# A bidirectional chunked scan: both directions' intra-chunk products in the first pass, the second pass with the state alone

## The reference, cut to what matters

```
xd    = x * dt[..., None]
a_cs  = cumsum(dt * a)                                   # in the chunk
decay = exp(where(tri, a_cs[l] - a_cs[s], -inf))
cb    = einsum("bclgn,bcsgn->bclsg", cc, bc)
y_diag = einsum("bclsgr,bcsgrp->bclgrp", cb * decay, xd) # inside a chunk
states = einsum(..., bc, exp(a_cs[-1] - a_cs), xd)       # what a chunk adds to the state
h      = h * exp(a_cs[-1]) + states                      # chunk after chunk
y_off  = einsum(..., cc, h_prev, exp(a_cs))              # what earlier chunks give
```

## Time and profile before

| | us |
|---|---|
| median of 3 runs | 4335.32 (4332.63 to 4337.5) |
| the profiled execution, its time | 4333.42 |
| its span | 4331.6 |
| `ssd_stage` in it, first to last instruction | 383.3 to 559.7 |

### The profile page before, as it was taken

One profiled execution on the slowest core, in us unless ns is written; L12 is line 12 of the kernel. 1 busy time (PEld: TensorE's weight loads), 2 busy tenths in 40 slices (PEclk: granted clock), 3 DMA queues, 4 the chain that ended last, 5 costly groups with the idle time before them and its releaser, 6 DMA issues. The chain is left out here.

```text
span 4331.6 us, 38016 instructions
## 1 busy us (share of the span) xinstructions
PE 3116.2 (72%) x12308; PEld 1334.8 (31%) x12308; DVE 2859.9 (66%) x7086; ACT 1130.9 (26%) x2975; POOL 1575.2 (36%) x1383
## 2 busy tenths in 40 slices
PE   8999999866667755555566658999877655555655
PEld 4656554422222211111122113565332211111111
DVE  2524765898888897555555555565888888555554
ACT  1122532333223222111222212563332322111111
POOL 0001413354554454444444441001445455444443
PEclk9999999988878887778778778999888877777677
DMA  4114858999999999999999994105999999999998
GB/s 175 39 39 138 276 187 319 390 420 415 420 420 399 420 421 420 419 421 414 410 419 418 420 417 190 39 1 199 395 420 420 416 421 417 421 421 419 419 421 336
DMA packets 223658, 1471.81 MB, mean 340 GB/s; under 512 B 25436, under 2 KB 29244, under 8 KB 53220
## 3 DMA queue, kind: packets, MB, share of 16 engines
q0 software_dynamic: 184320, 1342.26, 75.0%
q1 hardware_dynamic: 37764, 123.17, 7.9%
q10 hardware_dynamic: 1376, 3.96, 0.2%
HBM read 1467.02 MB, written 2.28 MB: 339 GB/s over the span
## 5 line engine op out<-in xcount | busy, mean ns | idle before, releaser
L1944 PE MATMUL banks<-arena 128*64 128x512 f32 x5120 | 1668.5, 812 | 1159.2 <-ACT arena L2188 1108.6
L1668 POOL DMA_INDIRECT arena<-experts,arena x1280 | 1498.9, 1171 | 2246.5 <-PE banks L1944 1535.3
L2341 DVE CUSTOM_DVE_ANT_0 arena<-arena 128x1024 f32<-128x1024 f32 x1280 | 1537.4, 1223 | 829.5 <-DMA arena<-experts,arena 828.9
L1944 PEld LDWEIGHTS banks<-arena 128*64 128x64 f32 x5120 | 457.5, 185 | 2297.1 <-ACT arena L2188 1295.1
L2182 ACT ACTIVATE arena<-arena 128x4 f32<-128x4 f32 x320 | 66.1, 206 | 2316.9 <-DVE arena L2341 2316.8
L2188 ACT ACTIVATE arena<-arena 128x64 f32<-128x64 f32 x1280 | 340.4, 336 | 37.5 <-DVE arena L2329 0.8
L1759 PE MATMUL banks<-arena 128*128 128x512 f32 (+3 forms) x960 | 289.4, 456 | 6.8 <-DMA arena<-wq 5.7
L442 PE MATMUL banks<-arena 128*128 128x512 f32 (+1 forms) x640 | 208.6, 486 | 0.3 <-PEq L207 0.3
L1759 PEld LDWEIGHTS banks<-arena 128*128 128x128 f32 x960 | 160.8, 191 | 116.3 <-issue 90.8
L879 POOL TENSOR_TENSOR arena<-arena 128x256 f32<-128x256 f32 x48 | 41.1, 856 | 423.5 <-POOLq L633 332.3
L1686 PE MATMUL banks<-arena 128*128 128x512 f32 x416 | 187.9, 600 | 5.9 <-DVE arena L2234 2.1
(11 more groups left out here) (245 smaller groups left out, 2970.5 us busy)
## 6 DMA issues: line engine op xcount, KB each, us to landing
arena<-l_w_ada SPq DMA_DIRECT2D x48, 1024.0 KB, 4.9
arena<-wq SPq DMA_DIRECT2D x54, 512.0 KB, 7.9
arena<-experts,arena POOLq DMA_INDIRECT x1280, 17.3
arena<-l_w_in SPq DMA_DIRECT2D x7, 2048.0 KB, 7.7
arena<-l_w_out SPq DMA_DIRECT2D x4, 1536.0 KB, 8.9
arena<-l_w_o SPq DMA_DIRECT2D x4, 1024.0 KB, 9.2
arena<-keys SPq DMA_DIRECT2D x27, 128.0 KB, 10.4
arena<-gates SPq DMA_DIRECT2D x6, 512.0 KB, 11.9
```

Source lines behind the costliest of these rows:

```text
L1668: pool.indirect_dma_start(slots[n], None, tbl, bass.IndirectOffsetOnAxis(ap=expert[:, ring[c], k:k + 1], axis=0)).then_inc(land[n]["sem"], ...
L1944: mm = pe.matmul(core["ps"][QS * j:QS * j + QS, c, :], diag[:, g % 2, k, :], v[:, D + c * 512:D + (c + 1) * 512], start=(g % (NB * PH) == ...
L2341: dve.tensor_tensor_reduce(u, u, rep[i // PH % 2][:, k % NQ, :], 1.0, 0.0, ALU.mult, ALU.add, dots[:, k:k + 1]).then_inc(dot["sem"], up(dot))
```

## The change

`steps` keeps its 48 entries, and the first 24 (the backward pass) now make the intra-chunk products of both directions; the forward pass is left with the state.

- `front(n)` exists for the 24 steps of the first pass only, is issued two steps ahead, and has one matmul of scores and two of sums, one per direction, into banks 0 and 1. Each bank has one buffer, so each waits for ACT's distance of the step before.
- ACT's `distance(n)` makes four Relu for each direction, into E (three buffers) and EF (one). The two distances are zero on opposite sides of the diagonal. POOL's `both(n)` adds them over 128x512, and ACT's `decay(n)` is then one Exp for both.
- DVE's `mask(n)` masks the scores twice. ACT's `scale_backward(n)` multiplies the backward scores by dt for four heads (Copy with a scale per partition). DVE's `weigh(n)` makes forward scores·dt + that (four SCALAR_TENSOR_TENSOR of 128x128), and one product with E in place. XD is gone: the product takes x itself.
- XE is x·(TOE·dt), with TOE·dt formed once on POOL at the start; closing steps make none.
- In the forward pass a step has the product with the state, the new state (into banks 2 and 3 in turn) and `add` without its last part.
- Four column groups are now done in the first pass, in six steps each (2, 1, 2, 1, 2 slices and the turn); the fifth has a slice in every other step of the forward pass, and is turned in step 40.

```diff
-    assert len(groups) * (KD + 1) <= NS
+    share = (2, 1, 2, 1, 2)
+    ada_at = {n: [] for n in range(NS)}
+    for q in range(len(groups) - 1):
+        for a, w in enumerate(share):
+            ada_at[6 * q + a] = [(q, sum(share[:a]) + b) for b in range(w)]
+        ada_at[6 * q + len(share)] = [(q, KD)]
+    for k in range(KD + 1):
+        ada_at[NW + 2 * k] = [(len(groups) - 1, k)]
...
+            def distance(n):
+
+                _r, t, g = steps[n]
+                for j, r in enumerate((1, 0)):
+                    act.wait_ge(fr["sem"], at(fr, 2 * n + j + 1))
+                    if j == 0 and n >= 3:
+                        act.wait_ge(bk["sem"], at(bk, n - 2))
+                    if j == 1 and n:
+                        act.wait_ge(ds_["sem"], at(ds_, n))
+                    o = EF if j else E[:, n % 3, :]
+                    for h in range(HG):
+                        c = r * HEADS + g * HG + h
+                        i = act.activation(o[:, h * P:(h + 1) * P], core["ps"][:, j, h * P:(h + 1) * P],
+                                           ACT.Relu, bias=KAC[:, t, c:c + 1], scale=-1.0)
+                    i.then_inc(dd["sem"], up(dd))
+
+            def scale_backward(n):
+
+                _r, t, g = steps[n]
+                act.wait_ge(cm["sem"], at(cm, 2 * n + 1))
+                if n:
+                    act.wait_ge(wg["sem"], at(wg, n))
...
+                    i = act.activation(SB[:, h * P:(h + 1) * P], CM[:, 2 * (n % 2), :], ACT.Copy,
+                                       scale=DT[:, t, c:c + 1])
+                i.then_inc(bs["sem"], up(bs))
+
+            def decay(n):
+
+                act.wait_ge(ds_["sem"], at(ds_, n + 1))
+                act.activation(E[:, n % 3, :], E[:, n % 3, :], ACT.Exp, scale=-1.0).then_inc(eo["sem"], up(eo))
+
+            distance(0)
+            scale_backward(0)
+            distance(1)
+            decay(0)
+            scale_backward(1)
+            for n in range(NS):
+                if n + 1 < NW:
+                    decay(n + 1)
+                if n + 2 < NW:
+                    distance(n + 2)
+                    scale_backward(n + 2)
...
+            def weigh(n):
...
+                for h in range(HG):
+                    c = g * HG + h
+                    i = dve.scalar_tensor_tensor(
+                        out=W[:, h * P:(h + 1) * P], in0=CM[:, 2 * (n % 2) + 1, :], scalar=DT[:, t, c:c + 1],
+                        in1=SB[:, h * P:(h + 1) * P], op0=ALU.mult, op1=ALU.add)
+                i.then_inc(wg["sem"], up(wg))
+                dve.wait_ge(wg["sem"], at(wg, n + 1))
                 dve.wait_ge(eo["sem"], at(eo, n + 1))
...
+                dve.tensor_tensor(E[:, n % 3, :], E[:, n % 3, :], W, ALU.mult).then_inc(mo["sem"], up(mo))
...
             mask(0)
+            mask(1)
+            weigh(0)
             for n in range(NS):
-                if n + 1 < NS:
-                    mask(n + 1)
+                if n + 2 < NW:
+                    mask(n + 2)
+                if n + 1 < NW:
+                    weigh(n + 1)
                 add(n)
...
+            def both(n):
+
+                pool.wait_ge(dd["sem"], at(dd, 2 * n + 2))
+                pool.tensor_tensor(E[:, n % 3, :], E[:, n % 3, :], EF, ALU.add).then_inc(ds_["sem"], up(ds_))
+
+            both(0)
+            both(1)
             for n, (r, t, g) in enumerate(steps):
...
+                if not closing[n]:
+                    c = r * HEADS + g * HG
+                    pool.tensor_tensor(per(XE[:, n % 2, :]), per(xs[:, t, g * GW:(g + 1) * GW]),
+                                       bcast(TOE[:, t, c:c + HG], HD), ALU.mult).then_inc(xe["sem"], up(xe))
+                if n + 2 < NW:
+                    both(n + 2)
...
             def front(n):
...
+                for j, r in enumerate((1, 0)):
+                    e = r * SG + g
+                    if n:
+                        pe.wait_ge(dd["sem"], at(dd, 2 * n - 1 + j))
+                    pe.matmul(core["ps"][:, j, :].rearrange("p (h l) -> p h l", l=P),
...
             front(0)
+            front(1)
             for n, (r, t, g) in enumerate(steps):
-                if n + 1 < NS:
-                    front(n + 1)
+                if n + 2 < NW:
+                    front(n + 2)
                 if n == 0:
                     stay_busy(pe, core, 6, 22)
...
+                if n < NW:
+                    pe.wait_ge(mo["sem"], at(mo, n + 1))
+                    for h in range(HG):
+                        a = g * GW + h * HD
+                        pe.matmul(core["ps"][:, 4 + n % 2, h * HD:(h + 1) * HD], E[:, n % 3, h * P:(h + 1) * P],
+                                  xs[:, t, a:a + HD], start=True, stop=True)
...
+                    pe.wait_ge(xe["sem"], at(xe, n + 2 - sum(closing[:n])))
+                    if 0 < n < NW:
                         pe.wait_ge(ac["sem"], at(ac, AC[n]))
```

More of the change, by code:

```diff
@@ L779, in _ @@
         def _(act):
[L780 to L783, removed]
-                for h in range(HG):
[L785 to L790, removed]
+            def distance(n):
[12 more added lines that the diff above has]
+                    i.then_inc(dd["sem"], up(dd))
@@ L840, in add @@
                             out=part(hs, h), in0=part(hs, h), scalar=CD[:, t, c + h:c + h + 1],
-                            in1=part(core["ps"][:, 6, 0:GW], h), op0=ALU.mult, op1=ALU.add)
+                            in1=part(state, h), op0=ALU.mult, op1=ALU.add)
                     i.then_inc(ac["sem"], up(ac))
-                if not opening[n]:
-                    dve.wait_ge(ac["sem"], at(ac, AC[n] + 1))
-                dve.tensor_tensor(yg, yg, core["ps"][:, 4 + n % 2, 0:GW], ALU.add).then_inc(ac["sem"], up(ac))
+                if n < NW:
+                    if not opening[n]:
+                        dve.wait_ge(ac["sem"], at(ac, AC[n] + 1))
+                    dve.tensor_tensor(yg, yg, core["ps"][:, 4 + n % 2, 0:GW], ALU.add).then_inc(ac["sem"], up(ac))
             def gate(u, j):
@@ L859, in _ @@
                         gate(gated_at[n - j], j)
[L860 to L867, removed]
@@ L868, in _ @@
-                if q < len(groups) and k == KD:
-                    dve.wait_ge(atr["sem"], at(atr, q + 1))
-                    ada_columns(dve, core, *groups[q], 7, ao)
+                for q, k in ada_at[n]:
+                    if k == KD - 1:
+                        dve.wait_ge(bl[q % 2]["sem"], at(bl[q % 2], 16 * (q // 2 + 1)))
+                        dve.wait_ge(am["sem"], at(am, (q + 1) * KD))
+                        if q:
+                            dve.wait_ge(st["sem"], at(st, 32 * sum(g > 0 for _l, g in groups[:q])))
+                        dve.tensor_tensor(ada_row, core["ps"][:, 7, :], ada_bias[q % 2],
+                                          ALU.add).then_inc(ar["sem"], up(ar))
+                    if k == KD:
+                        dve.wait_ge(atr["sem"], at(atr, q + 1))
+                        ada_columns(dve, core, *groups[q], 7, ao)
@@ L923, in _ @@
                 if not closing[n]:
-                    if n:
+                    pe.wait_ge(xe["sem"], at(xe, n + 2 - sum(closing[:n])))
+                    if 0 < n < NW:
                         pe.wait_ge(ac["sem"], at(ac, AC[n]))
-                    i = pe.matmul(core["ps"][:, 6, 0:GW], br[:, t, g * SN:(g + 1) * SN], XE[:, n % 2, :],
-                                  start=True, stop=True)
+                    i = pe.matmul(core["ps"][:, 6 if n < NW else 2 + n % 2, 0:GW], br[:, t, g * SN:(g + 1) * SN],
+                                  XE[:, n % 2, :], start=True, stop=True)
                 i.then_inc(bk["sem"], up(bk))
-                q, k = divmod(n, KD + 1)
-                if q < len(groups) and k < KD:
+                for q, k in ada_at[n]:
+                    if k == KD:
+                        pe.wait_ge(ar["sem"], at(ar, q + 1))
+                        ada_turn(pe, core, ada_row, 7).then_inc(atr["sem"], up(atr))
+                        continue
                     s, sig, v = plan[q * KD + k]
@@ L936, in _ @@
                     ada_slice(pe, core, ada_w[s], k, 7).then_inc(am["sem"], up(am))
-                if q < len(groups) and k == KD:
-                    pe.wait_ge(ar["sem"], at(ar, q + 1))
-                    ada_turn(pe, core, ada_row, 7).then_inc(atr["sem"], up(atr))
     close(core)
```

76 lines of the change are left out of this document (36 added, 40 removed).

## The result

The kernel after took 4353.7 us (4349.4 to 4356.0) against 4335.1 for the one before; the ratio is 1.0038, with an interval of 1.0028 to 1.0049. It is 18.6 us slower. The forecast was 4329 and the range 4320 to 4343, so the prediction has the wrong sign, and the time lies outside its range.

What follows compares the result with a forecast made beforehand. PE's order was taken to bound the stage, DVE second. Opening 12.0, first pass 112 and second pass 45.7 sum to 169.7 us against 176.4; with 0.4 for handoffs 6.3 less, 4329 on the median, range 4320 to 4343.

Steps and rivals of the forecast that it cites:

- the sum: Whole stage: 12.0 + 112 + 45.7 = 169.7 us against 176.4; 0.4 kept for handoffs, so 6.3 less.
- The rival of the clock: Second pass: TensorE's clock falls from step 41 on, PE having about 1.0 of 1.9 us; 4332 to 4345, chance 0.12.
- the rival's "2 to 3 us": Second pass, clock rival: the cost if only the last steps fall to the low clock; the whole pass would cost 16.
- its 112: First pass: four groups of 29.7 us, less 7.2 for work left out, plus 0.5 for handoffs.
- The opening: Stage start to first product: 12.0 us, 5.5 lost because the dummies stand behind the third front; first product at 395.3.
- The group of six steps: First pass: 26.5 us of PE work, 2.7 of load waits and 0.5 for DVE in the turn step, 29.7.
- The slice loads: First pass: loads land 4.9 us after issue, so the 3rd, 5th and 8th slice wait 0.9 each, 2.7 per group.
- The rival "the loads don't hold PE": First pass: a group of six falls to 27.6 us, 8.4 less in four groups; 4320, chance 0.2.
- four SCALAR_TENSOR_TENSOR of 128x128: DVE in each first-pass step: 1.05 us, within a DVE sum of 4.0 to 4.3 beside PE's 4.42.
- the rival of POOL's loop: First pass: `both` slowed by DVE sets the ACT-POOL loop, up to 6.0 us a step; 4341 to 4353, chance 0.15.
- its bound of 1.85: First pass: the loop stays under 4.95 us a step while `both` takes under 1.85; 1.3 was taken.
- The clock repairs itself: Second pass, argument against the clock rival: activity releases the throttled clock, and a slow PE is a busy one.

Runs made afterwards that it cites:

- second profile of the kernel after: The kernel after itself, unchanged, run again on another chip: 4348.8 us, ratio 1.0031 to the kernel before; its profiled span is 4341.9.
- the run with both edits: Kernel after with dummy matmuls in each group's three waiting slices and the opening's dummies spread between the fronts: 4335.1 us, ratio 0.9998 to the kernel before.

## Why the prediction was wrong, step by step

**The term that failed** is one that the sum doesn't name: each of PE's durations in opening and first pass was taken from rows at clock 1.00. The rival of the clock was there, and the earlier trace rows had its price, but it was looked for in the second pass alone, where PE has least to do, and given 0.12. The new waits (three in each group, four in the opening) were written into the sum as time only; nobody asked what they do to the clock. In the place where the rival stood, the clock did fall, near its end and for little: the profile has 0.96 in the second pass, and near 566 a product with the state takes 1.22 instead of 0.70. In the second profile of the kernel after, and in the runs with filled waits, moved dummies or both, the second pass has 0.91 to 0.93, and its first ten dummies (20 records) take 3.7 to 4.0 instead of 2.5. The second pass of that second profile takes 46.8 against 44.7, which is the rival's "2 to 3 us" for the last steps, not its 16.

**What it cost.** The first pass was 21 over its 112. With the waits filled it is 119, so 14 go (between two single executions) with the clock and 7 remain at full clock. The opening adds 1.6, and the dummies' 6.96 for 5.18 covers it. Against this stands 1.7 less in the second pass. The clock is not the whole miss: with opening and first pass at 1.00 the run with both edits is 1.0 under the kernel before, where the sum had 6.3.

**The group of six steps** was right as a total (29.70 and 29.39 at clock 1.00) and wrong in its parts by errors of opposite sign, so that the hit is luck: PE's work 25.2 (25.8 in the run with the moved dummies) for 26.5, and idle 3.9 for 2.7 and 0.5.

**The slice loads**: the 3rd, 5th and 8th slice wait, as derived. In the two groups at clock 1.00 that weren't filled they wait 1.24, 1.17 and 1.40, and 1.13, 0.97 and 1.17, for three times 0.9. In the second group of the first profile they wait 1.3, 0.9 and 2.7:

```profile
441.48 1.06 PE L139 MATMUL banks<-arena 128*32 128x512 f32 x8 [1.28 <-DMA arena<-l_w_ada]
...
447.36 1.06 PE L139 MATMUL banks<-arena 128*32 128x512 f32 x8 [0.92 <-DMA arena<-l_w_ada]
```

The 0.9 comes from the median landing of 4.9. The 8th slice's load is issued at 452.6 and lands 6.5 us later. The earlier trace rows had shown a maximum of 7.3, and the sum used the median alone. Why this one is late stays open. The next load, issued behind it at 456.53, doesn't explain it: in the second group of the second profile the next load follows just as closely (450.4 and 454.3), and the 8th slice's took 5.0. What both profiles do show is that two loads issued 0.9 us apart, at the start of the stage and of a group, don't land alike: the first took 4.7 to 5.0 and the second 6.3 to 7.2. The rival "the loads don't hold PE" is refuted.

**DVE**: four SCALAR_TENSOR_TENSOR of 128x128 take 1.13 for a forecast of 1.05; DVE is not the bound, though it is busy 27.7 and 28.1 in the two groups at clock 1.00 of 29.7 and 29.4. The Trainium skill, "Vector Engine (DVE) Microarchitecture Reference", section "Points that are easy to get wrong", says that a scalar-tensor-tensor with two SBUF sources that are not bf16 runs at half throughput. The trace doesn't show a halving for this form: four take 1.13 for twice the elements of the four that took 0.85 in the earlier trace rows, one source of which lies in PSUM.

**ACT and POOL.** Groups of the kernel after, by line and shape (line, engine, count | busy, mean ns | idle before and what ended it):

```profile
L943 POOL TENSOR_TENSOR arena<-arena 128x512 f32<-128x512 f32 x24 | 31.3, 1304 | 91.6 <-ACT arena L804 91.6
L816 ACT ACTIVATE arena<-arena 128x128 f32<-128x128 f32 x96 | 31.3, 427 | 3.7 <-DVE arena L867 3.7
...
L867 DVE SCALAR_TENSOR_TENSOR arena<-arena 128x128 f32<-128x128 f32 x96 | 28.2, 356 | 1.4 <-ACT arena L816 1.3
...
L823 ACT ACTIVATE arena<-arena 128x512 f32<-128x512 f32 x24 | 15.0, 626 | 3.9 <-POOL arena L943 3.8
```

`both` takes 1.304 for 1.3, and ACT's 24 Exps wait for it 3.8 us in all: the rival of POOL's loop is refuted, and its bound of 1.85 isn't reached. The four Copies take 1.31 instead of 1.14. No second table load appears. But the rival asked only what crossing costs POOL, and where DVE's 512-wide product starts just behind `both`, DVE pays more:

```profile
469.65 1.41 POOL L943 TENSOR_TENSOR arena<-arena 128x512 f32<-128x512 f32 x1 [3.52 <-ACT arena L804]
469.95 1.66 DVE L873 TENSOR_TENSOR arena<-arena 128x512 f32<-128x512 f32 x1
```

In this profile the product starts up to 0.4 us behind the addition five times out of 24, and then takes 1.6 to 1.8 for the 0.69 that it takes in most of the others. In the run without the slice loads it once started 0.25 ahead; there it took 0.69 and the addition 1.56. No run shows whether this reaches the end of a step.

**The clock repairs itself**: the Trainium skill, "TensorE: Matmul & The Clock Gate", section on the HAM clock gate, was quoted for the throttled clock as the default that activity releases. The trace agrees that it comes back (0.50 at 405.4 to 410, and 1.00 from 435.4 to 459.2). It doesn't follow that the loss is small: until then the time is gone, and a later wait brings the clock down again.

**What stays open**: the 7 us of the first pass at full clock (4 in its first three groups, 91.2 for 3 x 29.7 less 2.0, and 3 in the rest), of which some may be dummies that overrun their wait, since the filled groups take 30.0 and 31.1 and the unfilled ones at full clock 29.4 and 29.7; why single loads land late; and which of PE's pauses brings the clock down. The waits of 2.74, 3.00 and 3.37 shown or named here were each followed by half clock; in the second group of the run with the moved dummies, three waits of 1.2 to 1.4 left it at 1.00, and in the third group it fell some 2 us behind a wait of 1.35 (four products of 1.97 at 463.17).

## What to carry to other kernels

When an edit takes work from TensorE but leaves it waiting, price the wait twice: its own length, and the stretch behind it at half clock. Look for that at every new wait, not where the engine is least busy. Look at the clock beside the busy share, since a PE at half clock shows as full. If the wait can't be removed, fill it with matmuls into a free bank, or place the items that hang on transfers in steps long enough to hide them, one at a time.

## What the runs showed of the hardware

- 17 dummy matmuls (34 records) in each of four groups, put into waits, made the program 12 to 18 us of 4354 faster; the opening's 22 in another order 8 to 14.
- At a granted clock of 0.50 PE's work took nearly twice its time, the slice 1.94 for 1.06 and the four products 1.97 for 1.11, while ACT's eight Relus stayed at 2.17.
- The same program on the same inputs loses differently from run to run: clock 0.72, 0.90, 0.90 in one profile's groups, 0.80, 0.94, 1.00 in the other's.
- A 1 MB load issued 0.9 us behind another took 6.3 to 7.2 us to land, the one ahead of it 4.7 to 5.0. The median is not what a chain waits for.
- A 512-wide DVE product that started 0.05 to 0.4 us behind a 512-wide POOL addition took 1.6 to 1.8 us instead of 0.69; the addition took 1.27 to 1.51, for 1.27 alone.
